# One pass over the mixer heads of a two-block kernel: the normaliser in products of its own, heads placed anew, one weight load later

## The reference

```
proj = h @ w_in + b_in                    # split: xm, om, ip, fp, us, ga, gb
xc = silu(causal_dwconv(xm))              # 4 heads of 256
q, k = xc @ w_q, xc @ w_k                 # 128 wide;  v = xm
s   = (q k^T) * wmat                      # wmat: decay from ip and fp, stabilised by m_t
num = s v ;  den = rowsum(s)
h   = num / max(|den|, exp(-m_t))
hm  = standardize(h) * gain * sigmoid(om);  y_a = hm @ w_mlstm_down
ys  = gelu(s5_ssm(us));  val, gate = split(ys @ w_glu);  y_b = val * sigmoid(gate)
y   = (sigmoid(ga) * y_a + sigmoid(gb) * y_b) @ w_mix_out
```

## Time and profile before

| | us |
|---|---|
| median of three runs (range) | 1648.92 (1643.34 to 1650.2) |
| the profiled execution | 1648.92 |
| its span | 1647.1 |
| TensorE busy | 1510.0 (92%), granted clock 0.951 in the mean |
| VectorE, ScalarE, GpSimd busy | 887.5, 584.6, 645.0 (54%, 35%, 39%) |
| chain of waits | TensorE 31% of the span, VectorE 4%, ScalarE 1% in named lines |

### The profile page before, as it was taken

One profiled execution on the slowest core, in us unless ns is written; L12 is line 12 of the kernel. 1 busy time (PEld: TensorE's weight loads), 2 busy tenths in 40 slices (PEclk: granted clock), 3 DMA queues, 4 the chain that ended last, 5 costly groups with the idle time before them and its releaser, 6 DMA issues. The chain is left out here.

```text
span 1647.1 us, 19508 instructions
## 1 busy us (share of the span) xinstructions
PE 1510.0 (92%) x7136; PEld 1210.0 (73%) x7136; DVE 887.5 (54%) x1508; ACT 584.6 (35%) x857; POOL 645.0 (39%) x456
## 2 busy tenths in 40 slices
PE   4999988877999999996999899989994999999996
PEld 3776855666888878885878677768883888888885
DVE  4682368634876868477646245535646333332337
ACT  5332367215212122224334466344326332332231
POOL 2342210022565455463544323244632344445442
PEclk9999979888999999998899899899996999999998
DMA  7322100042465546221463533225322222222221
GB/s 270 96 77 77 45 27 2 1 166 84 170 214 191 205 153 218 102 77 45 160 131 109 153 135 135 96 88 195 116 75 77 97 82 102 103 95 108 79 103 51
DMA packets 48182, 185.70 MB, mean 113 GB/s; under 512 B 12961, under 2 KB 14113, under 8 KB 33249
## 3 DMA queue, kind: packets, MB, share of 16 engines
q1 hardware_dynamic: 30240, 165.53, 28.5%
q10 hardware_dynamic: 17856, 19.01, 4.2%
HBM read 169.71 MB, written 12.58 MB: 111 GB/s over the span
## 5 line engine op out<-in xcount | busy, mean ns | idle before, releaser
L1396 POOL TENSOR_TENSOR wlo<-raw,whi 128x512 fp32r<-128x512 f32 x448 | 639.3, 1459 | 969.6 <-ACT whi L892 969.6
L441 PE MATMUL bank<-Ahi,whi 128*128 128x512 f32 x1088 | 440.7, 405 | 21.8 <-issue 8.5
L443 PE MATMUL bank<-Ahi,wlo 128*128 128x512 f32 x1088 | 430.9, 396 | 0.0
L442 PE MATMUL bank<-Alo,whi 128*128 128x512 f32 x1088 | 430.8, 396 | 0.0
L892 ACT ACTIVATE whi<-raw 128x2048 fp32r<-128x2048 f32 x113 | 216.4, 1915 | 271.7 <-PE bank L471 217.0
L441 PEld LDWEIGHTS bank<-Ahi,whi 128*128 128x128 f32 x1088 | 209.3, 192 | 71.9 <-issue 18.0
L442 PEld LDWEIGHTS bank<-Alo,whi 128*128 128x128 f32 x1088 | 209.4, 192 | 45.0 <-issue 2.4
L443 PEld LDWEIGHTS bank<-Ahi,wlo 128*128 128x128 f32 x1088 | 208.6, 192 | 45.2
L469 PE MATMUL bank<-whi,Bhi 128*128 128x512 f32 x496 | 195.3, 394 | 5.9 <-POOL wlo L1396 5.9
L471 PE MATMUL bank<-whi,Blo 128*128 128x512 f32 x496 | 194.3, 392 | 0.0
L470 PE MATMUL bank<-wlo,Bhi 128*128 128x512 f32 x496 | 194.2, 392 | 0.0
(11 more groups left out here) (377 smaller groups left out, 1906.5 us busy)
## 6 DMA issues: line engine op xcount, KB each, us to landing
raw<-in_ws SPq DMA_DIRECT2D x113, 1024.0 KB, 4.9
adaw<-in_ada SPq DMA_DIRECT2D x48, 512.0 KB, 4.7
spill<-stage ACTq DMA_DIRECT2D x32, 256.0 KB, 2.0
X<-in_x SPq DMA_DIRECT2D x8, 512.0 KB, 6.2
gates<-spill SPq DMA_DIRECT2D x16, 256.0 KB, 5.4
w1k<-in_w1k SPq DMA_DIRECT2D x1, 2048.0 KB, 15.8
w1v<-in_w1v SPq DMA_DIRECT2D x1, 2048.0 KB, 20.1
XM<-spill ACTq DMA_DIRECT2D x8, 256.0 KB, 3.8
```

Source lines behind the costliest of these rows:

```text
L441: pe.matmul(ps[:], wh, hi[:, k], start=(k == 0), stop=False)
L442: pe.matmul(ps[:], wh, lo[:, k], start=False, stop=False)
L443: ins = pe.matmul(ps[:], wl, hi[:, k], start=False, stop=(k == kn - 1))
L1396: pool.tensor_tensor(wlo[slot][:, part], raw[slot][:, part], rd(whi[slot][:, part]), ALU.subtract).then_inc(sem("lo_split"), 1)
```

## The change

The normaliser den is no longer column 257 of each values product. `mlstm_values` makes 256-column products, two row blocks to a bank (pool O), and then the same sums again with the single column of ones, all into one bank of pool T; `values_out` and `head_rows` read them there. `HEAD_AT` becomes 13, 17, 22, 26; the positions of the q and k weights in the stream follow. Head 3 returns at k = 31. ScalarE does the silu of the next head before `head_rows`. The gate rows are made in one go ahead of the S5 states, AEC is turned at k = 6, and `run_outputs` waits for the states before its first product. The gelus come at k = 16 and 18, the `ys_part`s all in head 0. SyncE loads tile 69 no longer ahead of its waits.

```diff
-HEAD_AT = [12, 17, 22, 27]
+HEAD_AT = [13, 17, 22, 26]
...
@@ run_outputs
                 if half == 0:
                     pe.wait_ge(sem("toep_ready"), T.due("toep_ready", 4))
+                    pe.wait_ge(sem("xs_ready"), T.due("xs_ready"))
...
-                if half == 0:
-                    pe.wait_ge(sem("xs_ready"), T.due("xs_ready"))
...
@@ mlstm_values
+                for p in range(2):
+                    ps, where = bank("O")
+                    for i in range(2 * p, 2 * p + 2):
+                        for j in range(i + 1):
+                            at_ = [0, 512, 896, 1152][j] + (i - j) * P
+                            ins = pe.matmul(ps[:, i % 2 * ML_DV:(i % 2 + 1) * ML_DV], W[:, at_:at_ + P],
+                                            V[:, j, 0:ML_DV], start=(j == 0), stop=(j == i))
+                    done(ins, f"mn{h}.{p}", where)
+                ps, where = bank("T")
                 for i in range(NT):
-                    ps, where = bank("O" if i < 2 else "T")
                     for j in range(i + 1):
                         at_ = [0, 512, 896, 1152][j] + (i - j) * P
-                        ins = pe.matmul(ps[:, 0:ML_DV + 1], W[:, at_:at_ + P], V[:, j, :],
+                        ins = pe.matmul(ps[:, i:i + 1], W[:, at_:at_ + P], V[:, j, ML_DV:ML_DV + 1],
                                         start=(j == 0), stop=(j == i))
-                    done(ins, f"mn{h}.{i}", where)
+                done(ins, f"den{h}", where)
...
-                if k == 9:
+                if k == 6:
                     pe.wait_ge(sem("ifr_ready"), T.due("ifr_ready"))
-                    ps, where = bank("O")
+                    ps, where = bank("T")
...
                 if n == 0:
-                    mlstm_back(ML_H - 1)
                     pe.wait_ge(sem("B_ready"), T.due("B_ready", 8))
...
@@ ScalarE, the loop over SPILLED
-                if k in (15, 20):
-                    gelus(0 if k == 15 else 2)
-                    gelus(1 if k == 15 else 3)
+                if k in (16, 18):
+                    gelus(k - 16)
+                    gelus(k - 15)
                 for h, b in enumerate(HEAD_AT):
-                    if k == b + 6:
+                    if k == b + 6 or (k == len(SPILLED) and b + 6 >= k):
                         head_high(h)
...
                     if k == b + 4:
-                        head_rows(h)
                         if h < ML_H - 1:
                             silus(h + 1)
-            hi_upto(last_tile(INDEX["gv0"]) + 1)
-            head_high(ML_H - 1)
+                        head_rows(h)
...
@@ VectorE
-            gate_rows(1)
+            for part in (1, 2, 3):
+                gate_rows(part)
...
             run_states(0)
-            gate_rows(2)
             run_states(1)
             dve.sem_inc(sem("xs_ready"), 1)
-            gate_rows(3)
...
@@ SyncE
-            n_heads = n_s5 + 1
-            tiles(n_s5, n_heads)
+            n_heads = n_s5
             whole_spill()
```

More of the change, by code:

```diff
@@ L787, in mlstm_values @@
                 pe.wait_ge(sem("mw_ready"), T.due("mw_ready", NT))
+                for p in range(2):
[7 more added lines that the diff above has]
+                ps, where = bank("T")
                 for i in range(NT):
-                    ps, where = bank("O" if i < 2 else "T")
                     for j in range(i + 1):
                         at_ = [0, 512, 896, 1152][j] + (i - j) * P
-                        ins = pe.matmul(ps[:, 0:ML_DV + 1], W[:, at_:at_ + P], V[:, j, :],
+                        ins = pe.matmul(ps[:, i:i + 1], W[:, at_:at_ + P], V[:, j, ML_DV:ML_DV + 1],
                                         start=(j == 0), stop=(j == i))
-                    done(ins, f"mn{h}.{i}", where)
+                done(ins, f"den{h}", where)
             def mlstm_back(h):
-                for i in range(NT):
-                    pe.wait_ge(*taken(f"mn{h}.{i}"))
+                for p in range(2):
+                    pe.wait_ge(*taken(f"mn{h}.{p}"))
                 for c in range(2):
@@ L1211, in head_in @@
                     if h and c == 0:
-                        act.wait_ge(*full(f"mn{h - 1}.{NT - 1}"))
+                        act.wait_ge(*full(f"den{h - 1}"))
                     act.activation(V[:, :, c * P:(c + 1) * P], ps[:].rearrange("p (i c) -> p i c", i=NT),
@@ L1243, in head_rows @@
                 for i in range(NT):
-                    n = f"mn{h}.{i}"
-                    act.activation(H[:, i, :], bank_of(n)[:, 0:ML_DV], ACT.Identity, scale=sd[:, i:i + 1],
-                                   bias=nmr[:, i:i + 1]).then_inc(taken(n)[0], 1)
+                    ps = bank_of(f"mn{h}.{i // 2}")
+                    ins = act.activation(H[:, i, :], ps[:, i % 2 * ML_DV:(i % 2 + 1) * ML_DV], ACT.Identity,
+                                         scale=sd[:, i:i + 1], bias=nmr[:, i:i + 1])
+                    if i % 2:
+                        ins.then_inc(taken(f"mn{h}.{i // 2}")[0], 1)
             def head_high(h):
@@ L1294, in _ @@
                     act.wait_ge(sem("if_a"), A.did("if_a"))
-                if k == 4:
+                if k == 2:
                     act.wait_ge(sem("if_d"), A.due("if_d"))
@@ L1298, in _ @@
                     act.wait_ge(sem("if_a"), A.did("if_a"))
-                if k == 8:
+                if k == 3:
                     act.wait_ge(sem("if_d"), A.due("if_d"))
@@ L1304, in _ @@
                     toeplitz_groups()
-                if k == 10:
+                if k == 8:
                     act.wait_ge(*full("aec"))
@@ L2127, in values_out @@
                 for i in range(NT):
[L2128 to L2135, removed]
+                    if i % 2 == 0:
+                        dve.wait_ge(*full(f"mn{h}.{i // 2}"))
+                    ps = bank_of(f"mn{h}.{i // 2}")
+                    dve.bn_stats(st4[:, i, 0, :], ps[:, i % 2 * ML_DV:(i % 2 + 1) * ML_DV])
+                dve.wait_ge(*full(f"den{h}"))
+                den_ = bank_of(f"den{h}")[:, 0:NT]
+                stt(dd[:, 0:4], den_, -1.0, AEC[:, 1, :, h], ALU.mult, ALU.max).then_inc(sem("dve_step"), 1)
                 dve.wait_ge(sem("dve_step"), v.did("dve_step"))
+                tt(dd[:, 4:8], dd[:, 0:4], den_, ALU.max).then_inc(taken(f"den{h}")[0], 1)
+                dve.wait_ge(*taken(f"den{h}"))
                 dve.reciprocal(dd[:, 4:8], dd[:, 4:8]).then_inc(sem("dve_step"), 1)
@@ L2186, in _ @@
                 values_out(h)
-                if h < 2:
-                    ys_part(2 * h)
-                    ys_part(2 * h + 1)
+                if h == 0:
+                    ys_part(0)
+                    ys_part(1)
                 if h < ML_H - 1:
@@ L2193, in _ @@
                 head_out(h)
+                if h == 0:
+                    ys_part(2)
+                    ys_part(3)
             head_low(ML_H - 1)
```

## The result

The changed kernel takes 1677.03 us (median of 4 runs, 1673.12 to 1679.55) against 1647.75 us (1643.34 to 1650.2) before: a ratio of 1.0178, 95% interval 1.0161 to 1.0197, so 29 us slower. The forecast was 1666, with a range up to 1676. The direction was right, the size fell short by 11 us.

What follows compares the result with a forecast made beforehand. The prediction took TensorE, busy for 92% of the span, as the bound. Its terms summed to +17.4 us on the profiled 1648.92, giving 1666.3 us, forecast as 1666 with a range of 1653 to 1676.

Steps and rivals of the forecast that it cites:

- normaliser's products: TensorE, each head: 20 one-column instructions, 80 in all, at 0.111 us each for loading weights; +8.9 us.
- wait for xs_ready: TensorE ahead of the state products: later states and an earlier wait, 0 to 4.0 us, taken as +1.0.
- head 0 one chunk later: Start of head 0: one chunk more done by the q and k copies; -4.0 us, bounds -5 and -2.
- return of head 0: TensorE waits 2.3 us for H and 1.6 for XC(1), with half clock; +4.7 us.
- head 1: Silu and its table load stand ahead of H: TensorE waits 2.3 us, then half clock; +5.0 us.
- head 2: Return of head 2: idle time and half clock fall from 9.7 to 5.8 us; -3.9 us.
- end of the heads: After the last head, tile 69's late load and conversion hold gv0's copy and md0's bank; +5.7 us.
- ahead of the changed stretch: TensorE before the stretch the diff touches: forecast 0.
- The end of the heads: Rival: head 3's earlier return pays, -7.1 instead of +5.7 us, if tile 69 is converted in time; 1653.5 us; chance 0.10.
- cheap columns: Rival: narrow products take 0.07 us each and new 2.3 us waits leave the clock alone; 1657.4 to 1660 us; chance 0.14.
- The clock falls at every normaliser: Rival: 2.2 us of nearly empty products act like a wait in every head, about +9 us; 1675 us; chance 0.10.

Runs made afterwards that it cites:

- e2: Changed kernel with gate rows 2 and 3, their ScalarE steps and the aec transposes back in their old places, early xs_ready wait kept: 1664.45 us.
- e3: Kernel before, with only TensorE's wait for xs_ready moved ahead of the TOEG products: 1649.92 us, ratio 1.0001.
- e1: Changed kernel with TensorE's wait for xs_ready put back behind the TOEG products, gate rows still ahead of the states: 1670.46 us.
- e4: Changed kernel with the xs_ready wait still behind chunk 8, but chunk 9 ahead of both halves of the state products: 1672.55 us.
- e5: Changed kernel with weight tile 69 issued again ahead of SyncE's wait for the end of the heads: 1665.25 us.
- e7: Changed kernel with the normaliser inside products of 257 columns again, nothing else undone: 1680.71 us, ratio 1.0181.
- e6: Changed kernel with ScalarE's head_rows(h) ahead of silus(h + 1) again: 1679.76 us, ratio 1.0189.
- e10: Kernel before, with the normaliser's own products in a row as its only edit: 1663.43 us, ratio 1.0092.
- e9: Changed kernel with ScalarE's silus(h + 1) one chunk earlier: 1673.92 us, ratio 1.0156.
- e14: Changed kernel; gate rows, xs_ready wait, tile 69 as before; own normaliser products in heads 0, 2 only; silus a chunk earlier; XC split before roots' wait: 1639.03 us.
- e11: Changed kernel with gate rows, xs_ready wait, tile 69 and ScalarE's order as before, normaliser's own products in heads 0 and 2 only: 1646.92 us.
- e15: Kernel before, with each one-column normaliser product set directly ahead of the 256-column product with the same weights: 1658.33 us, ratio 1.0057.

## Why the forecast was right or wrong

By the prediction's own terms, in the profiled executions (us; stretches of TensorE from one milestone to the next):

| term | forecast | measured |
|---|---|---|
| normaliser's products | +8.9 | +9.2 |
| wait for xs_ready | +1.0 | +13.6 |
| head 0 one chunk later | -4.0 | -4.6 |
| return of head 0 | +4.7 | +5.5 |
| head 1 | +5.0 | +7.0 |
| head 2 | -3.9 | -6.6 |
| end of the heads | +5.7 | +4.4 |
| ahead of the changed stretch | 0 | -2.3 |

They sum to +26.2; the spans differ by 25.3. The last row is no effect of the change: 2.0 of it are there at the first 32-column product (L731), which starts anywhere from 807.6 to 813.2 us in the profiled executions.

**The step that failed** is the wait for xs_ready: "A wait of 0 to 4.0 ... I take +1.0". It left its own bounds at three points. The states start 10.2 us later against TensorE, not 6.6: part 3 of the gate rows, on 4 partitions, takes 1.83, 2.19 and 1.60 us an operation, which I had not counted one by one. They meet a little less of GpSimd's split, as forecast (30.6 us in all, against 34.8 with 1.9 of moved steps in them), and the wait is 5.54. And I put no clock behind it, though I had priced half clock behind every other new wait over 2 us, at 2.7; here it was 8.0 (6.7 in the products, 1.3 in the chunk), as 64-column products run behind it. From 883.08 to 909.54 TensorE takes 26.5 us; before it was 12.9. e2 shows the term (-12.6 us without the late states), e3 that the early wait alone costs nothing, e1 that the late states alone cost 6 to 7, and e4 how much of the rest is the clock: wide products behind the same wait lose 2.9 instead of 8.0.

**The rest held in sum, in part by luck.** Forecast without the failed term +16.4, measured +14.9, or +12.6 with the 2.3 us of noise ahead of it. The waits for H came as said (1.97, 2.21, 1.98 for 2.3), the wait for XC at 1.62 for 1.6, md0 10.06 for 10 to 11 with tile 69's load ahead; e5 shows that last cause. But head 1 cost 2.0 more, 1.5 of it the clock behind the normaliser, and head 2 came out 2.7 lower: behind its wait of 1.98 half clock took 1.5 instead of 2.7, and the 0.8 for q's copy was gone. These two cancel. Head 0's -4.6 came by another path: the forecast wait of 2.7 for XC isn't there, but one of 2.23 for a chunk's bank, which was in no step, with 1.7 of half clock behind it. ScalarE's copy is late, as it issues twelve transfers ahead of it, from 925.39 to 934.88; e2, whose states are in time, has that wait as well (2.55).

**Right size, incomplete reason:** in the sum the normaliser is a price alone and ScalarE's order a price alone. e7 and e6 give neither back: taken out, the one brings a wait of 7.40 us for a bank, the other one of 3.26 for XC. The joint sum was not wrong by this, but it says nothing on what undoing a part is worth.

**The rivals.** The end of the heads did not pay; cheap columns fell: by the trace the product of one column costs 0.1075 us an instruction. By the Trainium skill ("TensorE: Matmul & The Clock Gate", "LDWEIGHTS (loading the stationary operand)") a load takes its columns divided by 1.2 in ns, an estimated 107 ns for 128, and this trace agrees. The floor of about 25 ns of its "Back-to-back issue gap" didn't show here, where each product loads weights. "The clock falls at every normaliser" gave 1675, next to the measured time, but by one head of four in the profile; it is the true account of e10, where all four fell.

## What to carry over

Before a wait is moved ahead of work that used to cover it, add up the producer's new queue operation by operation, and price the wait by what runs behind it: narrow products at half clock doubled the bill of a 5.5 us wait, wide ones behind the same wait lost 2.9 us. Where two heads are four chunks apart, three things meet in one place (a bank, H, XC); undoing one edit only hands the wait to the next, so such edits are tried together. A sum of terms can be right and still not tell what each edit is worth alone.

## What the hardware showed beyond that

A row of 20 one-column products, 2.15 us with TensorE never idle, was followed by a slow chunk (over 7.1 us instead of 5.5 to 5.7) in 20 of the 42 heads of the twelve profiled executions that have one (the changed kernel, e1, e2, e4, e5, e6, e9 to e14): in all four of e10, one of four in the changed kernel, none of two in e11. Head 1's was slow in all nine that have it. What decides it stays open. Set between the wide products they were not, in none of e15's four heads. After a wait of 1.98 us (e1) and one of 5.54 us (changed kernel) the 64-column products ran at half clock to their end, 7.0 and 14.0 us long.
